# Hybrid retention/attention encoder layer on one core: the last projection taken tile by tile, with routing and slot placement under it

## The reference, cut to what matters

```python
m = sigmoid(gr) * y_r + sigmoid(gd) * y_d
x = x + einsum('btd,de->bte', m, w_out)            # the last projection, 1024 x 1024
...
# hier_moe(rmsnorm(x, g_ffn)): best group of 4, then the best 2 of its 4 experts
g_logits = xf @ w_group + b_group
g_idx = argmax(g_logits);  g_w = softmax(g_logits)[g_idx]
e_sel = (xf @ w_expert + b_expert) of the chosen group
top_v, top_i = top_k(softmax(e_sel), 2);  top_v = top_v / sum(top_v)
for e in range(16):
    he = silu(xt @ w_gate[e]) * (xt @ w_up[e])     # D_FF = 512
    y = y + combine[:, e:e + 1] * (he @ w_down[e])
```

## Time and profile before

| | |
|---|---|
| median of 3 runs | 1123.05 us (1121.44 to 1124.24) |
| profiled execution, its own time | 1120.21 us |
| its span, first to last instruction | 1118.4 us |
| PE, DVE, ACT, POOL busy | 93%, 58%, 45%, 15% |
| mean granted PE clock | 0.966 |

### The profile page before, as it was taken

How to read it: one execution, slowest core, us unless ns; L and a number is a source line. 1 busy time by engine, 2 the same in 40 slices (tenths; PEclk the granted TensorE clock), 3 DMA queues, 4 the chain that set the end, 5 groups by cost and what they waited for, 6 DMA issues and landing times.

```text
span 1118.4 us, 12130 instructions
## 1 busy us (share of the span) xinstructions
PE 1035.6 (93%) x4816; PEld 837.1 (75%) x4816; DVE 645.7 (58%) x794; ACT 499.7 (45%) x665; POOL 164.8 (15%) x172
## 2 busy tenths in 40 slices
PE   4999999999999989999999999992399999999994
PEld 3788887887776767778777888882278888888883
DVE  4677764134334343234337555427978898989880
ACT  3532333344445344332343222134258787877761
POOL 1000020110211201111111000000102231313121
PEclk9999999999999999999999999995599999999998
DMA  9243364462542604423347432219689999999972
GB/s 295 61 137 119 122 212 153 159 204 67 193 133 103 225 30 151 148 92 114 131 178 261 147 131 72 85 51 347 243 292 357 377 405 384 403 383 397 390 276 41
DMA packets 58945, 225.66 MB, mean 202 GB/s; under 512 B 5088, under 2 KB 5136, under 8 KB 46464
## 3 DMA queue, kind: packets, MB, share of 16 engines
q1 hardware_dynamic: 38000, 149.97, 35.8%
q0 software_dynamic: 20880, 74.83, 20.6%
HBM read 189.12 MB, written 35.65 MB: 201 GB/s over the span
## 4 chain that ended last, share of the span: by engine, by line
PE 87%; DVE 5%; DMA 3%; ACT 2%; issue 1%; POOL 1%; SPq 0%; ACTq 0%; DVEq 0%; POOLq 0%
PE ps L385 22%; PE ps L386 22%; PE ps L387 22%; PE ps L1517 3%; PE ps L1518 3%; PE ps L1531 2%; PE ps L1495 2%; DMA q_tok<-z_q 2%; PE ps L1665 2%; PE ps L1568 2%; PE ps L1597 1%; PE ps L1765 1%; DVE onehot L1416 1%; PE ps L1648 1%; DMA raw<-in_w_in 1%
## 5 line engine op out<-in xcount | busy, mean ns | idle before, releaser
L385 PE MATMUL ps<-w_hi,s_hi 128*128 128x512 f32 x704 | 282.8, 402 | 2.4 <-ACT stage L766 1.1
L387 PE MATMUL ps<-w_lo,s_hi 128*128 128x512 f32 x704 | 275.7, 392 | 0.0
L386 PE MATMUL ps<-w_hi,s_lo 128*128 128x512 f32 x704 | 275.5, 391 | 0.0
L385 PEld LDWEIGHTS ps<-w_hi,s_hi 128*128 128x128 f32 x704 | 133.1, 189 | 31.7 <-issue 2.1
L387 PEld LDWEIGHTS ps<-w_lo,s_hi 128*128 128x128 f32 x704 | 133.0, 189 | 28.3
L386 PEld LDWEIGHTS ps<-w_hi,s_lo 128*128 128x128 f32 x704 | 133.2, 189 | 27.9 <-issue 1.0
L766 ACT ACTIVATE stage<-ps,x_rstd 128x512 f32<-128x512 f32 x64 | 44.0, 689 | 218.1 <-PE ps L387 218.1
L357 DVE TENSOR_TENSOR w_lo<-raw,w_hi 128x2048 fp32r<-128x2048 f32 x44 | 100.7, 2289 | 50.1 <-ACT w_hi L352 49.9
L352 ACT CAST w_hi<-raw 128x2048 fp32r<-128x2048 f32 x44 | 83.6, 1907 | 14.1 <-DMA raw<-in_w_in 8.7
L672 POOL DMA_INDIRECT out_y<-y_exp,s_idx x16 | 46.2, 2890 | 210.9 <-ACT y_exp L967 210.9
L373 DVE TENSOR_TENSOR lo_x<-raw_x,w_hi 128x2048 fp32r<-128x2048 f32 x32 | 71.9, 2284 | 4.4 <-ACT w_hi L368 4.4
(11 more groups left out here) (281 smaller groups left out, 1746.0 us busy)
## 6 DMA issues: line engine op xcount, KB each, us to landing
raw<-in_w_in SPq DMA_DIRECT2D x32, 1024.0 KB, 7.8
raw_x<-in_w_up SPq DMA_DIRECT2D x30, 1024.0 KB, 12.1
raw_x<-in_w_down SPq DMA_DIRECT2D x18, 1024.0 KB, 11.8
raw<-in_w_gate SPq DMA_DIRECT2D x16, 1024.0 KB, 11.6
raw_x<-in_w_gate SPq DMA_DIRECT2D x16, 1024.0 KB, 11.8
raw<-in_w_down SPq DMA_DIRECT2D x14, 1024.0 KB, 11.5
raw<-in_w_diff_o SPq DMA_DIRECT2D x4, 1024.0 KB, 5.9
raw<-in_w_ret_o SPq DMA_DIRECT2D x4, 1024.0 KB, 6.5
```

Source lines behind the costliest of these rows:

```text
L385: nc.tensor.matmul(out, s_h, w_h, start=first, stop=False)
L386: nc.tensor.matmul(out, s_l, w_h, start=False, stop=False)
L387: return nc.tensor.matmul(out, s_h, w_l, start=False, stop=last)
```

## The change: what it does

**Order of the last projection.** `x` = 4 and 5 are done tile by tile: `dense(4, t)`, `dense(5, t)`, then the next tile, in the order 0, 1, 2, 3, PT. All four weight blocks are therefore held until the last tile; blocks 42 and 43 (`LAST` and the next) go to slots of their own, with hi parts over space of the gates, and are loaded earlier. The experts' first 12 blocks use the slots in another order and wait for other things.

**Routing tile by tile.** The transposes of the tile before go into the middle of a product (`route`, after k = 3), its logits between the tile's two products. DVE has `choose` (18 small operations) between the two residual additions and `place_rows` (9) before them. ACT has the square and root (`root_x2`) and the exponentials (`exps`) of each tile.

**Scatter in place of one-hots and gather.** Every token's normed row, with its number and 16 weights beside it (`rows_out`, 1056 wide), is scattered by POOL to the slots of its two experts in a DRAM tensor `x_slots` (two indirect DMAs a tile). An expert then loads 128 rows by a plain DMA (`load_rows`). `x_slots` is filled with empty rows early, by four DRAM-to-DRAM copies of 4 x 128 rows (2.16 MB each) and a small one, in SP's queue behind the loads of blocks 4 to 8. The 16 one-hots, `slot_rhs`, the gather and the store of h2 are gone. The stores of x2 to y move from POOL to SP, one for each tile.

```diff
+CAP = TT * P
+XW = D_MODEL + 32
+ORDER = (0, 1, 2, 3, PT)
...
     def split_hi(act, j, i, q):
...
+            act.wait_ge(blocks_used, LAST - 1 + RAW_ORDER[m] if m >= 2 else LAST - 2)
+        else:
+            act.wait_ge(logits_ready, TT)
...
+            if 4 <= n < 4 + NG:
+                e = EPG * (n - 4)
+                sp.dma_start(x_slots[e * CAP:(e + EPG) * CAP, :].rearrange("(e c) x -> e c x", e=EPG)[:, 0:P, :],
+                             a["c_empty"].unsqueeze(0).to_broadcast([EPG, P, XW])).then_inc(slots_empty, 16)
...
+                if m < 2:
+                    sp.wait_ge(blocks_used, LAST - 2)
+                elif m < WR + 2:
+                    sp.wait_ge(blocks_used, LAST - 1 + m - 2)
                 elif m == 6:
+                    sp.wait_ge(p_evacuated, TT * OUT_CHUNKS - 1)
+                elif m == 7:
                     sp.wait_ge(p_evacuated, TT * OUT_CHUNKS)
...
+                elif m == 8:
+                    sp.wait_ge(y_init, 16 * (TT + 1))
+                    for k in range(2):
+                        sp.wait_ge(x_loaded[k], 16)
...
+        for n, t in enumerate(ORDER):
+            rows = P if t < PT else SAMPLE
+            pool.wait_ge(row_ready, n + 1)
+            for k in range(2):
+                pool.indirect_dma_start(out=x_slots,
+                                        out_offset=bass.IndirectOffsetOnAxis(ap=dest[0:rows, t, k:k + 1], axis=0),
+                                        in_=rows_out[0:rows, t, :], in_offset=None).then_inc(dispatched, 16)
+        pool.wait_ge(dispatched, 16 * 2 * TT)
...
+        dense_hi(act, LAST + 1)
+        source_hi(3, PT)
+        for n, t in enumerate(ORDER):
+            if n:
+                root_x2(ORDER[n - 1])
+                source_hi(4, ORDER[n - 1])
+            if t == PT:
+                lower_half_of(4)
+                lower_half_of(5)
+            if n >= 3:
+                split_hi(act, 0, 0, n - 1)
+            if n:
+                exps(ORDER[n - 1])
+        source_hi(4, ORDER[PT])
+        root_x2(ORDER[PT])
         split_hi(act, 0, 0, 4)
+        exps(ORDER[PT])
...
+        for n, t in enumerate(ORDER):
+            if n:
+                source_lo(4, ORDER[n - 1])
+            if n >= 2:
+                place_rows(ORDER[n - 2])
+            evacuate_out(4, t)
+            if n:
+                root_of_tile(ORDER[n - 1])
+                choose(ORDER[n - 1])
+            evacuate_out(5, t)
+            if n:
+                rows_of_tile(ORDER[n - 1])
+            if n >= 3:
+                split_lo(dve, 0, 0, n - 1)
+        place_rows(ORDER[PT - 1])
+        source_lo(4, ORDER[PT])
+        root_of_tile(ORDER[PT])
+        rows_of_tile(ORDER[PT])
+        choose(ORDER[PT])
+        place_rows(ORDER[PT])
         split_lo(dve, 0, 0, 4)
...
+        def route(n):
+            if n == 0:
+                next_source(3, PT)
+            else:
+                next_source(5, ORDER[n - 1])
+            if n >= 2:
+                positions(n - 2)
...
+        for n, t in enumerate(ORDER):
+            dense(3, IN_CHUNKS + 4, t, p_ready, within=n)
+            if n:
+                logits(ORDER[n - 1])
+            dense(3, IN_CHUNKS + 5, t, p_ready)
+        positions(PT - 1)
+        next_source(5, ORDER[PT])
+        logits(ORDER[PT])
+        positions(PT)
+        pe.wait_ge(row_ready, TT)
```

More of the change, by code:

```diff
@@ L133, in build @@
     fold = after("fold", [SAMPLE, COLS], f32)
[L134 to L140, removed]
+    gen = after("gen", [P, 3 * P + TT + 2 * NE + 1], f32)
+    ident, tri, ones = (gen[:, i * P:(i + 1) * P] for i in range(3))
+    tok_id = gen[:, 3 * P:3 * P + TT]
+    base16, rank16 = (gen[:, 3 * P + TT + i * NE:3 * P + TT + (i + 1) * NE] for i in range(2))
+    pad_row = gen[:, 3 * P + TT + 2 * NE:3 * P + TT + 2 * NE + 1]
     gret, gsub = after("gret", [P, DV], f32), after("gsub", [P, DV], f32)
@@ L150, in build @@
     lam = after("lam", [P, 4], f32)
+    eps = after("eps", [P, 1], f32)
+    x2_rms = after("x2_rms", [P, 2, TT], f32)
     x_rstd = after("x_rstd", [P, TT], f32)
@@ L249, in build @@
     y_exp = (y_exp0, y_exp1)
+    slot_w = at("slot_w", [P, NE], f32, X + 57344)
+    s_idx = after("s_idx", [P, NE], u32)
+    left = after("left", [P, NE], f32)
+    slot_row = after("slot_row", [P, NE], f32)
+    slot_at = after("slot_at", [P, NE], u32)
+    assert end[0] <= X + 58880
     ps = nc.alloc_psum_tensor("ps", [P, 8, COLS], f32)
@@ new lines, in _ @@
+        place_rows(ORDER[PT - 1])
[4 more added lines that the diff above has]
+        place_rows(ORDER[PT])
+        split_lo(dve, 0, 0, 4)
+        split_lo(dve, 0, 0, 5)
+        dve.wait_ge(pos_ready, TT + 1)
+        totals = ps[:, 7, TT * NE:(TT + 1) * NE]
+        own(v.tensor_reduce(cmax[:, 0:1], totals, AX.X, ALU.max))
+        for k in range(1, TT):
+            own(v.tensor_scalar(cmax[:, k:k + 1], cmax[:, 0:1], float(P * k), None, ALU.is_gt))
@@ L1472, in _ @@
         expert_pass(0)
-        assert own.n == before + LIST_STEPS + COUNT_STEPS
+        assert own.n == before
         passes = dve.value_load(npass[0:1, 0:1], min_val=1, max_val=TT)
@@ L1496, in source, with dense @@
                 last.then_inc(src_transposed, 1)
-        def dense(s, c, t, ready):
-            u = TT * c + t
+        def dense(s, c, t, ready, within=None):
+            x = c - IN_CHUNKS
+            u = TT * c + t if x < 0 else TT * IN_CHUNKS + out_unit(x, t)
+            ends = t == (ORDER[-1] if x >= 4 else PT)
             pe.wait_ge(slo_ready, 2 * TT * s + 2 * (t + 1))
@@ L1518, in dense @@
                     last = mm(bank, s_hi[:, k, rows], w_l, start=False, stop=k == KC - 1)
-                    if kk == 3:
-                        last.then_inc(blocks_used, 1)
-            if t < PT:
+                if ends and kk == 3:
+                    last.then_inc(blocks_used, 1)
+                if k == 3 and within is not None:
+                    route(within)
+            if not ends:
                 last.then_inc(ready, 1)
@@ L1721, in logits, with positions @@
             last.then_inc(logits_ready, 1)
-        for x in range(OUT_CHUNKS):
+        def positions(n):
+            pe.wait_ge(sel_ready, n + 1)
+            if n:
+                pe.wait_ge(row_ready, n)
+            out = ps[:, 7, ORDER[n] * NE:(ORDER[n] + 1) * NE]
+            for s in range(n + 1):
+                last = mm(out, (tri16 if s == n else ones16)[:, :], sel[:, ORDER[s], :], start=s == 0, stop=s == n)
+            last.then_inc(pos_ready, 1)
+        def route(n):
+            if n == 0:
+                next_source(3, PT)
+            else:
+                next_source(5, ORDER[n - 1])
+            if n >= 2:
+                positions(n - 2)
+        for x in range(4):
             for t in range(TT):
```

531 lines of the change are left out of this document (261 added, 270 removed).

## The result

The change makes the kernel slower: a median of 1143.85 us (4 runs, 1139.91 to 1145.76) against 1122.24 us (4 runs, 1120.25 to 1124.24) before. The ratio is 1.019, with a 95% interval of 1.015 to 1.022. The prediction was 1110.8 us, 12 us faster, with 6% for slower. The profiled execution after has an own time of 1143.23 us and a span of 1141.4 us.

The account below looks back on a forecast made before the run. PE bounds the kernel, nearly idle at half clock in the 55.0 us before the experts. First expert product at 761.0 + 35.0 = 796.0 against 808.2 wins 12.2: 1123.0 - 12.2 = 1110.8 us, own range 1107 to 1115.

Parts of the forecast that it names:

- In front: Term 0, bound +2: Dense part: four fills in SP's queue, each 5.6 to 12.8 us, delay weight loads without cost, at worst 2 us.
- PE loses 4e - 52: Chunks from 50 to 120 us: PE's loss from block 8 standing behind four fills of e us each.
- Rival 4: Slow fills before the experts: at 16 us each all 12.2 us are lost, at 19 the time is 1135; 6%.
- A: End of the last dense product: from 753.2 to 761.0 us, by 5.0 of moved work and waits of 1.8 and 1.0.
- S - A: Sample tile's chain from last dense product to first expert product: 35.0 us, against 55.0 before.
- behind S: From the first expert product (S, forecast 796.0 us) to the end: 310 us left alone, term 0.
- The wait at `route(0)`: Middle of the last projection's first product: PE waits 1.8 us for a PSUM bank that DVE's lo parts free.
- the one before the logits of tile 3: Last projection: PE waits 1.0 us for tile 3's lo parts, 5.6 us on DVE against PE's 4.7.
- the first scatter beside the splits: Sample tile's first scatter on POOL, as two DVE splits start: 2.8 us, taken from a gather beside one split.
- the lower bounds: Sample tile's chain: shortest landing times, 3 us for the scatter and 3.5 for the load of the rows.
- rival 3: Experts: DMA never catches up 4 MB of later weight loads, 6.7 us reach PE, time 1117.5; 12%.
- The rule of the Trainium skill that I weighed: ACT's ten table switches: 26.6 us instead of 12.8, an estimated 3 us more in A; left out of the sum.

Follow-up runs that it names:

- the first run: The changed kernel with the four fills' dimensions swapped, 128 rows outermost and four experts inside: 1108.57 us, ratio 0.989 to the kernel before.
- waiting splits: The kernel of the first run, with DVE's two last splits of expert weights held until all ten scatters have landed: 1106.62 us, ratio 0.986.

## Why the prediction was wrong

**The step that failed** is "In front: Term 0, bound +2", and in it the price of a fill. I took 5.6 us from a rate of 387 GB/s as the one end and 12.8 us from the h2 store as the other, "however far". Both rows are of transfers with 128 rows outermost. A fill in this shape takes some 20 us: 19 to 20 by its rate, 20.6 to 21.9 by its packets. Fed with e = 20, my own line "PE loses 4e - 52" gives 28 us; the windows show 28.7 of idle time up to 180 us, and the fold is 34 late. The 5 to 6 us between are the matmuls at the lower clock behind each hole, for which the line has no term. That 28 and 28.7 are so near is in part luck: the line is for block 8 alone and lets its load be issued at once, but in the changed kernel that load is issued at 111.53 us, and PE had lost time to blocks 5, 6 and 7 before. Rival 4, at 6%, was this mechanism, and its price at e = 19, 1135 us, is 9 below the median. So the mechanism stood in the rival, and the forecast had its term at 0: its size and its chance were wrong. With the good shape (e = 6.0 us) a term of 0 was right, and the time became 1108.6, which is 12.3 us under its own before, where I had 12.2. So near a hit is luck: A comes 1.9 later behind the fold than forecast, S - A is 2.2 shorter, and behind S there are 2.0 more.

**A.** Predicted 65.1 us behind the fold at 695.88, measured 65.4. The wait at `route(0)`, predicted 1.8, is 1.4; the one before the logits of tile 3, predicted 1.0, is 0.65. PE has no third wait in the projection (busy 64.43 of the 66.50 us from 728.9 on), so no gap in a full tile. The 1.6 us for `sel` at 796.99 stand behind A, beside DVE's chain, where they cost nothing. As the two waits are 0.75 shorter than predicted and the sum is 0.3 longer, the work itself took 1 us more.

**S - A.** Step by step behind A, predicted and measured in the changed kernel: addition done +3.4, +2.8; lo parts +9.8, +8.7; logits +11.8, +10.7; rows placed +18.3, +17.0; second scatter starts +22.3, +22.5; landed +26.8, +26.1; first rows in +31.6, +30.0; product +35.0, +33.4. Taken one by one, most terms are 0 to 0.9 us too large. One was too small, by 1.5: for the first scatter beside the splits I took 2.8 from the gather, and it took 4.89, about as long as both splits. The gather's row had only one split beside it, and ended 0.8 us behind it, as the scatter ends 0.8 behind the second of its two. The short landing, 3.59 for the scatter and 3.62 for the load, lies between the plain load's 4.5 and the lower bounds.

**Behind S.** Term 0 was wrong by 2 us, but not for the reason of rival 3. ACT's waits for weights are 0.3 us at most in the first run, and the start of the last `down` product comes sooner after the first expert product than before (289.5 us against 291.1). That product itself takes 7.4 us instead of 5.8, so the last scatter starts as late as before: 298.4 us behind S in the changed kernel, 298.5 before. The 2 us lie behind it. From the start of the last scatter to the end of the span it is 14.1 us against 11.7 before, 13.7 and 14.2 in the first run and with waiting splits, and 11.2 and 11.6 in the two kernels before with fills. It belongs to the changed code, and no run here tells what it is; this stays open.

**The rule of the Trainium skill that I weighed**, on the page "ScalarE: Activation LUTs", section "What ACT_TABLE_LOAD costs", expected a drain of about 1380 ns with each table load. The timeline of ACT after has

```profile
786.24 1.28 ACT L920 ACT_TABLE_LOAD   x1
787.54 0.30 ACT L920 ACTIVATE x_rms<-stat,eps 128x1 f32<-128x1 f32 x1
```

with an operation before it that ends at 786.23, so there is no drain of 1.38 us on either side of it, and the row's value was the right one.

**The rule that I should have weighed** stands on the page "DMA: Bandwidth & Descriptors" of the Trainium skill, section "Why a DMA increments its semaphore by 16 and not by 1": a DMA is dealt out to the largest number of engines up to 16 that divides the slowest dimension of both sides. The traces agree in all four shapes tried: from 57 to 62 us the DMA share is 0.27 with 4x11x12288 and 0.27 with 4x128x1024, but 1.05 with 128x4x1056 and 0.94 with 16x8448.

## What to carry to other kernels

Price a new DMA by its shape as the compiler leaves it, not by its bytes: one with 4 outermost moved 109 to 115 GB/s where one with 128 outermost moved some 360. Then count what stands behind it, in its queue and on its engines. Where a term has no row, and the nearest rows differ from it in the one respect that may matter, the range must go beyond them. What a change does as a side job, far from the place it is about, deserves as much working as its core.

## What the runs showed that I had not expected

- A DMA copy kept four of sixteen engines busy for 20 us, and moving such copies to a queue of their own, spread out in time, took away only a part of the loss (1131 us, against 1144 in the loads' queue and 1109 in the good shape).
- Copying within DRAM is about as fast as what runs beside it: some 360 GB/s of engine time, where the loads and the store from 50 to 75 us in the kernel before have 347 (132 GB/s at a share of 0.38). 8.7 MB of it hid entirely beside the dense part.
- POOL's indirect scatter of 64 rows took 4.89 us beside two splits of DVE and 0.90 without; two plain loads issued by POOL took 1.13 beside a split and 1.12 without. The Trainium skill, "SBUF — State Buffer", section "SBUF: two separate sides", says that a DVE operation with two SBUF inputs holds a shared port for its whole length against a GpSimd operation that reads SBUF. The trace agrees: a split has two such inputs (`raw`, `w_hi`), the indirect DMA has its row numbers in SBUF (`dest`), and it ends 0.8 us behind the split. That these row numbers are the reason why it is held and the plain loads are not is a reading; no run isolates it.
